# A state-space output projection by seven block products in a stage of its own, behind one chain of 32 scan chunks

## The chip, the cores and the metric

The kernel runs on one core of one Trainium2 chip. The metric is the device time of one execution in microseconds, as the median of repeated runs. All data is float32.

## The reference, cut to what matters

The program is a two-layer decoder trunk with 1,024 tokens and width 1,024. Layer 0 is attention with pooling and an FFN, layer 1 a state-space mixer (SSD) and an FFN. The change lies in the mixer of layer 1 and in what follows it:

```python
y = ssd_chunked(xs, dt, A, Bm, Cm) + xs * D[:, None]     # 8 chunks of 128 tokens, 4 groups of 8 heads
y = y.reshape(b, s, SSD_INNER) * silu(z)                  # SSD_INNER = 2048
yg = y.reshape(b, s, SSD_GROUPS, 512)
yg = yg * rsqrt(mean(yg * yg, axis=-1) + EPS)             # one root for each token and group
x = x + (yg.reshape(b, s, 2048) * norm_w) @ w_out         # the output projection, 1024 x 2048 x 1024
x = x + swiglu(rmsnorm(x, ffn_norm_w[1]), ...)            # the second FFN
```

## The kernel before, in words

**Products.** A float32 product is made of three TensorE products of float32r parts: high by high, high by low, low by high. The high part is a copy by ScalarE (`w_hi`, `y_hi`, `s_hi`, `d_hi`), the low part the difference to it, taken by GpSimd (`w_lo`, `s_lo`) or VectorE (`y_lo`, `d_lo`). The large projections (both FFNs, and the state-space input in `q_stage`) already run as seven block products in place of eight (M1 to M7: each operand is cut into 2 x 2 blocks, sums of blocks are multiplied, and each result is added to the output blocks that `ADDS_TO` names).

**Order.** Each engine has one queue of instructions, written out by hand in five blocks (SyncE, GpSimd, ScalarE, TensorE, VectorE), with semaphores between them. An instruction that waits holds all behind it on its engine.

**A group of the mixer (`ssd_group(g)`, g = 0 to 3).** `load_rows` brings back B, C (`bc_rows`) and x (`yx`) of the group, 1.5 MB in two halves of 512 tokens, from the scratch tensor `conv_rows`. The scan goes over NT = 8 chunks c. `token_major(c+1)` makes C times B (`CB`) and turns x; VectorE makes `cbm`, `btok` and `xdt` of it; GpSimd makes `xds`. TensorE then makes the states, `yoff`, and `ydiag` (L2592), for which it waits for the masked decay `mdec`. `mdec` is loaded 512 KB a chunk (`load_decay`, two buffers, behind `ydiag` of the chunk before the last), and worked on by ScalarE (`eacs`, relus, exponentials) and VectorE. VectorE adds up y (L3385, counted by `y_ready`). After each chunk TensorE makes one or two z halves (`z_half`, 12 products each, 16 a group: the gate projection of the group), ScalarE takes silu of z, VectorE multiplies it into y (`gated`).

**The projection now.** At the end of each group the gated y is squared (ScalarE), summed over four blocks (GpSimd, L1205), and over channels (`square_sums`, L2606). `split` and `lo` make `y_hi` and `y_lo`. `out_part` makes 16 output halves (8 tiles of 128 tokens, two halves of 512 columns), each of 4 blocks x 3 products (L1925 to L1927), and `add_out` (L2679) scales each by the root of its tokens and adds it to `xres`. The root is a column that fits tokens on partitions. Loads of the next group's rows and weights (`load_piece`, `w_raw`) run in this stretch. In the last group the products go in `TILE_ORDER`, and from the sixth output half on `ffn_T` puts the norm's transposes for the second FFN between them, so the tiles of x are complete one after the other.

**The down projection and the q stage**, which the new stage resembles: `down_slice` (L2298 to L2306) makes 12 products of one `s` block (`hidden`, through DRAM) and one `d` block (weights), in a ring of five buffers; its last additions (L2926) are followed by the norm (`plain`, L2691), transposes (L2003) and block sums of the q stage.

Of the kernel before, what the change touches and what calls it, by code (L numbers as in the profile page):

```python
# [33 lines left out]
P = 128  # L34
# [37 lines left out]
class Order:  # L72


    def __init__(self, names):
        self.at = {name: i + 1 for i, name in enumerate(names)}
        assert len(self.at) == len(names)
        self.total, self.seen = len(names), 0

    def count(self, layer, *name):  # L80
        return layer * self.total + self.at[name]

    def step(self, layer, *name):
        self.seen += 1
        assert self.seen == self.count(layer, *name), (self.seen, layer, name)
# [4 lines left out]
TILE_ORDER = (0, 1, 2, 4, 3, 5, 6, 7)  # L90
NEXT_PAIR = ("M2g", "M5g", "M6g", "M3g", "M7g", "M1u", "M4g", "M2u", "M5u", "M6u", "M3u", "M7u")


def trunk(nc, x, mix_norm_w, ap_w_in, ap_sinks, pool_w, pool_scale, ap_w_out, ssd_w_in, ssd_conv_w,
# [40 lines left out]
    with ExitStack() as ctx:  # L135
# [17 lines left out]
        slot5_at = [nc.sbuf_base - SPLIT_SLOTS * 4 * DM, nc.sbuf_base]  # L153
# [12 lines left out]
        scratch = small[:, 173:174]  # L166

# [22 lines left out]
        def f(ap):  # L190
# [36 lines left out]
        y_hi = at("y_hi", 0, [BG, S], F32R)  # L227

        sq = [[at(f"sq{h}{b}", b * S + BANK if h == 0 else 4 * S + b * BANK, [BANK]) for b in range(BG)]
              for h in range(2)]  # L230
        zs = [at(f"zs{b}", b % 2 * BANK, [BANK], origin=slot5_at[b // 2]) for b in range(BG)]

        yx = at("yx", 8 * S, [BG, S])
        y_lo = at("y_lo", 8 * S, [BG, S], F32R)


        def unit_at(name, unit, start, shape, dt=F32):
            return at(name, unit * DM + start, shape, dt, origin=weights_at)

# [4 lines left out]
        xs_n = [unit_at(f"xs_n{i}", 8 + i, 0, [DM]) for i in range(2)]  # L244
        bc_raw = [unit_at(f"bc_raw{i}", i, 0, [NK, P]) for i in range(2)]
# [60 lines left out]

        rows_v = at("rows_v", 0, [2 * NK, S], origin=xn_at)
        t1_val = at("t1_val", NK * S, [H2, S], origin=xn_at)
        d12 = [rows_v[:, p_, 0:BANK] for p_ in range(NP)]
        d22 = [rows_v[:, p_, BANK:] for p_ in range(NP)]  # L310
        d21 = [rows_v[:, NP + p_ % 5, p_ // 5 * BANK:(p_ // 5 + 1) * BANK] for p_ in range(NP - 1)]
# [3 lines left out]
        conv_rows = nc.dram_tensor("conv_rows", (G * NCB, P, S), F32, kind="Internal").ap()  # L315
        decay_sums = nc.dram_tensor("decay_sums", (G, NT, HG * P), F32, kind="Internal").ap()
# [15 lines left out]
        def turn_banks(layer, q):  # L332
# [310 lines left out]
        def _(sp):  # L643
# [207 lines left out]
            def ssd_group(g):  # L851
# [49 lines left out]
                if g == 0:  # L901
                    load_back(6, 7)
# [2561 lines left out]
```

## Time and profile before

| | |
|---|---|
| Median of 3 runs | 2283.26 us (2281.89 to 2283.43) |
| Profiled execution | 2282.14 us |
| Its span | 2280.4 us |
| TensorE busy | 2258.5 us, 99% |
| VectorE, ScalarE, GpSimd busy | 1320.3, 1101.5, 1320.6 us |
| Moved by DMA | 281.45 MB, mean 123 GB/s |

The span runs from the first to the last instruction that the profiler saw; the profiled execution's own time is 1.7 us longer. The ends of matmuls are modelled, so a busy TensorE need not be at its full pace. The mixer's groups lie between about 1160 and 1649 us, each 118 us apart; the second FFN follows.

### The profile page before, as it was taken

The numbers are of one execution on the slowest core, as the hardware profiler recorded it, in microseconds if no ns is written. First come the engines' busy times: TensorE is split into PE (matmuls) and PEld (weight loads), VectorE is DVE, ScalarE is ACT, GpSimd is POOL, SyncE is SP. The second block draws the span as 40 slices with busy tenths as digits, with TensorE's granted clock in tenths as the row PEclk, the third lists the DMA queues.
The fourth block names the chain that finished last, engine by engine and source line by source line (L and its number), as shares of the span: only waits on it lengthen the run. The fifth ranks groups of instructions, "written<-read, shape, count | busy, mean of one in ns | idle before, by whom it ended". The sixth has DMA issues, their size and how long they took to land.

```text
span 2280.4 us, 28960 instructions
## 1 busy us (share of the span) xinstructions
PE 2258.5 (99%) x10698; PEld 1845.5 (81%) x10698; DVE 1320.3 (58%) x1716; ACT 1101.5 (48%) x2016; POOL 1320.6 (58%) x950
## 2 busy tenths in 40 slices
PE   8999999999999999999999999999999999999998
PEld 6877888888888878888878888888888888888887
DVE  7357663333335798855568484747854343336777
ACT  4046544333333446655567474737643333334445
POOL 3224288777774664787734242334388777774654
PEclk9999999999999999999999999999999999999999
DMA  5100323323227855233263323232222323228744
GB/s 164 47 28 19 120 64 112 120 88 120 88 102 259 268 161 166 93 112 119 86 222 123 120 84 118 86 102 93 102 88 97 122 84 122 85 106 292 250 148 155
DMA packets 170807, 281.45 MB, mean 123 GB/s; under 512 B 19232, under 2 KB 104108, under 8 KB 168108
## 3 DMA queue, kind: packets, MB, share of 16 engines
q1 hardware_dynamic: 167084, 267.68, 34.9%
q10 hardware_dynamic: 3584, 11.93, 1.3%
q8 instruction: 86, 1.41, 0.3%
q14 instruction: 53, 0.43, 0.1%
HBM read 209.71 MB, written 69.86 MB: 123 GB/s over the span
## 4 chain that ended last, share of the span: by engine, by line
PE 92%; DVE 3%; POOL 2%; issue 1%; ACT 1%; DMA 1%; SPq 0%; ACTq 0%; DVEq 0%; POOLq 0%
PE ps L2212 44%; PE ps L1925 8%; PE ps L1927 8%; PE ps L1926 8%; PE ps L2302 5%; PE ps L2306 5%; PE ps L2298 5%; PE ps L2592 1%; PE ps L2582 1%; PE ps L2575 1%; PE ps L1948 1%; PE ps L2370 1%; POOL sq L1205 1%; PE ps L2135 1%; PE ps L2168 1%
## 5 line engine op out<-in xcount | busy, mean ns | idle before, releaser
L1051 POOL TENSOR_TENSOR s_lo<-s_val,s_hi 128x512 fp32r<-128x512 f32 x154 | 235.5, 1533 | 196.7 <-ACT s_hi L1575 196.0
L2862 DVE TENSOR_TENSOR xres<-ps,xres 128x512 f32<-128x512 f32 x132 | 90.5, 688 | 400.2 <-PE ps L2212 400.2
L947 POOL TENSOR_TENSOR w_lo<-w_raw,w_hi 128x1024 fp32r<-128x1024 f32 x50 | 119.3, 2387 | 270.6 <-ACT w_hi L1239 205.9
L972 POOL TENSOR_TENSOR p_lo<-p_val,p_hi 128x512 fp32r<-128x512 f32 x176 | 239.4, 1369 | 48.6 <-ACT p_hi L1380 37.5
L1380 ACT ACTIVATE p_hi<-p_val 128x512 fp32r<-128x512 f32 x176 | 111.0, 632 | 307.8 <-POOL p_val L998 307.8
L2212 PE MATMUL ps<-xn_hi,p_hi 128*128 128x512 f32 x704 | 189.0, 390 | 1.2 <-ACT xres L1483 1.2
L2212 PE MATMUL ps<-xn_lo,p_hi 128*128 128x512 f32 x704 | 188.2, 389 | 0.0
L2212 PE MATMUL ps<-xn_hi,p_lo 128*128 128x512 f32 x704 | 188.2, 389 | 0.0
L1575 ACT ACTIVATE s_hi<-s_val 128x512 fp32r<-128x512 f32 x154 | 97.0, 630 | 160.8 <-DMA d_val<-in_w_down 89.9
L1925 PE MATMUL ps<-xn_hi,w_hi 128*128 128x512 f32 x400 | 160.3, 401 | 0.0
L1926 PE MATMUL ps<-xn_lo,w_hi 128*128 128x512 f32 x400 | 156.0, 390 | 0.0
L1927 PE MATMUL ps<-xn_hi,w_lo 128*128 128x512 f32 x400 | 155.9, 390 | 0.0
L2212 PEld LDWEIGHTS ps<-xn_hi,p_hi 128*128 128x128 f32 x704 | 131.5, 188 | 28.9 <-ACT p_hi L1380 2.0
L2212 PEld LDWEIGHTS ps<-xn_lo,p_hi 128*128 128x128 f32 x704 | 132.1, 188 | 27.5
L2212 PEld LDWEIGHTS ps<-xn_hi,p_lo 128*128 128x128 f32 x704 | 132.2, 188 | 27.5
L2302 PE MATMUL ps<-d_lo,s_hi 128*128 128x512 f32 x560 | 151.3, 390 | 1.0 <-DVE d_lo L2914 0.8
L2298 PE MATMUL ps<-d_hi,s_hi 128*128 128x512 f32 x560 | 151.0, 390 | 0.0
L2306 PE MATMUL ps<-d_hi,s_lo 128*128 128x512 f32 x560 | 150.7, 389 | 0.0
L2914 DVE TENSOR_TENSOR d_lo<-rows_v,d_hi 128x512 fp32r<-128x512 f32 x108 | 126.3, 1173 | 21.7 <-ACT d_hi L1578 21.6
L1483 ACT ACTIVATE xres<-ps 128x512 f32<-128x512 f32 x132 | 77.8, 591 | 113.8 <-PE ps L2212 113.8
L1239 ACT ACTIVATE w_hi<-w_raw 128x1024 fp32r<-128x1024 f32 x48 | 50.0, 1051 | 159.9 <-PE ps L1927 154.4
L2302 PEld LDWEIGHTS ps<-d_lo,s_hi 128*128 128x128 f32 x560 | 104.7, 188 | 24.6 <-DVE d_lo L2914 3.1
(361 smaller groups left out, 5570.3 us busy)
## 6 DMA issues: line engine op xcount, KB each, us to landing
s_val<-hidden SPq DMA_DIRECT2D x154, 256.0 KB, 2.9
hidden<-xres SPq DMA_DIRECT2D x20, 1792.0 KB, 6.5
wv_g<-in_w_gate SPq DMA_DIRECT2D x22, 1024.0 KB, 5.2
wv_u<-in_w_up SPq DMA_DIRECT2D x20, 1024.0 KB, 5.1
d_val<-in_w_down SPq DMA_DIRECT2D x70, 256.0 KB, 4.1
rows_v<-in_w_down SPq DMA_DIRECT2D x64, 256.0 KB, 3.8
mdec<-decay_sums SPq DMA_DIRECT2D x32, 512.0 KB, 4.2
xres<-parked_x SPq DMA_DIRECT2D x24, 512.0 KB, 6.0
```

The costliest lines, as they stand in the source:

```text
L947: pool.tensor_tensor(w_lo[piece.slot][:, :], raw[piece.raw][:, :], f(w_hi[piece.slot][:, :]), ALU.subtract).then_inc(lo_done, 1)
L972: pool.tensor_tensor(p_lo[n][:, :, :], src, f(p_hi[n][:, :, :]), ALU.subtract).then_inc(p_lo_done, 1)
L1051: pool.tensor_tensor(s_lo[i][:, :], s_val[i][:, :], f(s_hi[i][:, :]), ALU.subtract)\
L1380: act.activation(p_hi[n][:, :, :], src, ACT.Copy).then_inc(p_hi_done, 1)
L1925: pe.matmul(dst, l_hi, r_hi, start=first, stop=False, skip_group_check=reopened)
L1926: pe.matmul(dst, l_hi, r_lo, start=False, stop=False, skip_group_check=reopened)
L1927: return pe.matmul(dst, l_lo, r_hi, start=False, stop=last, skip_group_check=reopened)
L2212: ins = pe.matmul(bank, l_[:, k, :], r_[:, k, :], start=first and k == 0, stop=last and k == H2 - 1, skip_group_check=reopened)
L2298: pe.matmul(banks[t_], s_hi[i][:, t_ * P:(t_ + 1) * P], d_hi[i][:, :], start=p == 0, stop=False)
L2302: pe.matmul(banks[t_], s_hi[i][:, t_ * P:(t_ + 1) * P], d_lo[i][:, :], start=False, stop=False)
L2306: pe.matmul(banks[t_], s_lo[i][:, t_ * P:(t_ + 1) * P], d_hi[i][:, :], start=False, stop=False)\
L2914: dve.tensor_tensor(d_lo[i][:, :], down_operand(DOWN[j], p, i), f(d_hi[i][:, :]), ALU.subtract).then_inc(d_lo_done, 1)
```

## The change

- **Products.** The projection moves behind all four groups. It is made of seven block products of eight pairs of blocks (`OUT_SEQ`, 56 slices of 12 products, `out_slice`). The token blocks are two halves of 512 tokens, the channel blocks pairs of 128, the columns two halves of 512.
- **y through DRAM.** The root is now applied before the projection: `square_sums` makes it as four rows of 128 tokens, `root_row` stores the 2 KB row and loads it back as 128 x 512 (`rr`), `row_normed` multiplies, `mix` makes the four sums of blocks on VectorE (S1 to S4), and `store_blocks` writes the seven kinds of y block to `gated_y` (14 stores of 256 KB a group). `load_out` loads each slice's y block and weight block (one to three loads of 256 KB) into a ring.
- **One chain of 32 chunks.** `token_major(k+1)` of the next group stands in the last chunk of the group before. Gates, norms, sums and stores of a group lie in the next group's chunks; those of the last group lie behind chunk 31, while slices 0 to 8 (M1 and M2 of other groups' blocks) are at TensorE. z goes in other orders, two to three halves after each chunk, and none after the last.
- **x.** It stays parked in DRAM through the mixer and comes back in eight loads of 512 KB (`load_x_back`) during the first slices.
- **Entry into the second FFN.** `second_entry` and `second_T` put the norm's first four transposes between slices of M3, and the other four between products of the FFN. Tiles 4 to 7 are complete after the last slice.
- The q stage's semaphores are merged with the FFN's (`q_full` into `product_full`, and so on), with the same waits.

```diff
-        ssd_slots = [[0, 3, 1, 2, 4, 0, 3, 1], [2, 0, 1, 3, 4, 2, 0, 1], [3, 0, 1, 2, 4, 3, 0, 1], [2, 1, 3, 0, 4, 2, 1, 3]]
+        ssd_slots = [[0, 3, 1, 2]] * G
+        OUT_SEQ = ([(0, p) for p in range(6)] + [(1, p) for p in range(3)] + [(0, p) for p in (6, 7)]
+                   + [(1, p) for p in range(3, NO)] + [(j, p) for j in range(2, 7) for p in range(NO)])
+        Z_AFTER_CHUNK = [[(5,), (6, 7), (8,), (9,), (10, 11), (12, 13), (14,), (15,)],
+                         [(0, 1), (2, 3), (4, 5), (6, 7), (8, 9), (10, 11), (12, 13), (14, 15)],
+                         [(0, 1), (2, 3), (4, 5), (6, 7), (8, 9), (10, 11), (12, 13), (14, 15)],
+                         [(0, 1, 2), (3, 4), (5, 6), (7, 8), (9, 10), (11, 12, 13), (14, 15), ()]]
@@ SyncE @@
+            def load_decay(k):
+                g, c = k // NT, k % NT
+                if k >= 2:
+                    sp.wait_ge(ydiag_full, k - 1)
+                sp.dma_start(mdec[c % 2]..., decay_sums...).then_inc(decay_loaded[c % 2], 16)
+            def root_row(n):
+                sp.wait_ge(rms_ready, n + 1)
+                sp.dma_start(rr_rows[n], rinv[0:4, :]).then_inc(rr_stored, 16)
+                sp.wait_ge(rr_stored, 16 * (n + 1))
...
+                sp.dma_start(rr[n % 2][:, :], rr_rows[n:n + 1]...to_broadcast([P, BANK])).then_inc(rr_loaded, 16)
+                load_piece(g, 3)
+                for c in range(NT):
+                    if NT * g + c + 2 < NT * G:
+                        load_decay(NT * g + c + 2)
+                    if c == 0 and g:
+                        root_row(2 * g - 2)
...
+                    if c == 2 and g:
+                        first_stores(g - 1)
...
+                    if c == 4 and g:
+                        sp.wait_ge(y_stored, 16 * (14 * (g - 1) + 4))
+                        root_row(2 * g - 1)
...
+                    if c == 6:
+                        if g:
+                            sp.wait_ge(y_normed, BG * 2 * g)
+                            store_blocks(g - 1, "M1", "M2")
+                            sp.wait_ge(mix_ready, 8 * (g - 1) + 4)
+                            store_blocks(g - 1, "M7")
+                        else:
+                            sp.wait_ge(gc_ready, 1)
+                        if not last:
+                            load_xrows(g + 1, 0)
+                            load_bc(g + 1, 0)
+                            load_piece(g + 1, 2)
+                    if c == 7:
+                        if g:
+                            sp.wait_ge(mix_ready, 8 * g)
+                            store_blocks(g - 1, "M6", "M3")
+                            sp.wait_ge(y_stored, 16 * 14 * g)
+                        if not last:
+                            load_xrows(g + 1, 1)
+                            sp.wait_ge(ydiag_full, NT * (g + 1))
+                            load_bc(g + 1, 1)
+            def out_loads(load_gate):
+                for s_ in range(2, 6):
+                    load_out(s_)
+                load_x_back(4)
+                load_out(6)
+                load_out(7)
+                load_x_back(0)
+                root_row(2 * G - 2)
+                load_x_back(5)
+                first_stores(G - 1)
+                sp.wait_ge(y_stored, 16 * (14 * (G - 1) + 4))
+                root_row(2 * G - 1)
+                load_out(8)
+                load_x_back(1)
+                sp.wait_ge(y_normed, BG * (2 * G - 1) + 2)
+                store_blocks(G - 1, "M1")
+                sp.wait_ge(y_stored, 16 * (14 * (G - 1) + 6))
+                load_out(9)
...
@@ TensorE @@
+            def token_major(k):
+                g, c = k // NT, k % NT
+                if c % 4 == 0:
+                    pe.wait_ge(rows_loaded[c // 4], 32 * (g + 1))
...
+                for c in range(NT):
+                    k, tok = NT * g + c, slice(c * P, (c + 1) * P)
+                    if k + 1 < NT * G:
+                        token_major(k + 1)
...
+            for s_ in range(OUTS):
+                out_slice(s_)
+                if s_ == 3:
+                    square_sums(2 * G - 1)
+                if o_at(6, 2) <= s_ <= o_at(6, 5):
+                    second_T(s_ - o_at(6, 2))
@@ the second FFN, TensorE @@
                 product(0, "M1g")
+                    second_T(4)
                 product(0, "M2g")
+                    second_T(5)
+                    second_T(6)
                 product(0, "M1u")
+                    second_T(7)
                 product(0, "M2u")
                 product(0, "M5g")
@@ VectorE @@
+                for c in range(NT):
+                    masked_decay(c)
+                    if k + 1 < NT * G:
+                        token_major(k + 1)
+                    if c == 0 and g:
+                        gated(g - 1, 1)
+                        reciprocal_rms(2 * g - 2)
+                    if c == 2 and g:
+                        for b in range(BG):
+                            row_normed(g - 1, b, 0)
+                        for i in range(2):
+                            mix(g - 1, "S1", i)
+                    if c == 4:
+                        gated(g, 0)
+                        if g:
+                            reciprocal_rms(2 * g - 1)
+                    if c == 6 and g:
+                        for b in H1_ORDER:
+                            row_normed(g - 1, b, 1)
+                        for i in range(2):
+                            mix(g - 1, "S3", i)
+                    if c == 7 and g:
+                        for name in ("S2", "S4"):
+                            for i in range(2):
+                                mix(g - 1, name, i)
+                    if c >= 6 and last:
+                        out_low(c - 6)
...
+            gated(G - 1, 1)
+            reciprocal_rms(2 * G - 2)
+            out_low(2)
+            out_low(3)
+            for b in range(BG):
+                row_normed(G - 1, b, 0)
+            for i in range(2):
+                mix(G - 1, "S1", i)
+            out_low(4)
+            reciprocal_rms(2 * G - 1)
+            out_low(5)
+            for b in H1_ORDER:
+                row_normed(G - 1, b, 1)
+            for name in ("S3", "S2", "S4"):
+                for i in range(2):
+                    mix(G - 1, name, i)
+            ffn(1)
@@ VectorE, end of second_entry @@
+                    for t_ in range(4):
+                        add_result("M3", t_, 4, 1)
+                    for q in range(4, NT):
+                        make(q)
+                    for i in range(4):
+                        tail_t1(i)
+                        tail_t2(i)
+                        tail_t3(i)
+                        tail_b22(i)
+                    for i in range(4):
+                        tail_lo1(i)
+                    for i in range(4):
+                        tail_t4(i)
+                        tail_lo2(i)
```

## Rows read from the trace of the kernel before

**Rows 1.** The page's head and busy times of the engines.

```profile
span 2280.4 us, 28960 instructions
...
PE 2258.5 (99%) x10698; PEld 1845.5 (81%) x10698; DVE 1320.3 (58%) x1716; ACT 1101.5 (48%) x2016; POOL 1320.6 (58%) x950
```

**Rows 2.** Windows: us, busy us (x instructions) of PE, PEld, DVE, ACT, POOL, PEclk, DMA share, GB/s.

```profile
1252.00:1370.00 118.00, 117.47 (x654) 95.86 (x653) 72.74 (x128) 68.60 (x136) 42.36 (x27) 1.00 0.30 99
...
1291.00:1349.00 58.00, 58.00 (x382) 46.65 (x381) 42.84 (x86) 44.18 (x91) 24.49 (x17) 1.00 0.37 122
...
1606.00:1713.00 107.00, 106.31 (x504) 87.95 (x503) 72.57 (x87) 59.23 (x109) 66.44 (x47) 1.00 0.26 91
```

**Rows 3.** Groups of instructions, TensorE, 1252.2 to 1370.3: busy us, mean ns, idle before.

```profile
L1925 PE MATMUL ps<-w_hi,y_hi 128*128 128x512 f32 x65 | 25.6, 394 | 0.0
...
L2606 PE MATMUL ps<-small,sq 128*128 128x1 f32 x16 | 2.0, 246 | 0.5 <-POOL sq L1205 0.5
```

**Rows 4.** The chain of work, 350 to 700: start, us, what.

```profile
350.21 348.42 PE ps L2212 x1536
```

**Rows 5.** The chain of work, 1290 to 1350: ydiag of chunks 1 and 2.

```profile
1302.05 1.02 PE ps L2592 x16
...
1311.26 1.02 PE ps L2592 x16
```

**Rows 6.** Timeline, VectorE, 1347 to 1356: start, us, operation.

```profile
1351.04 3.97 DVE L3396 SCALAR_TENSOR_TENSOR y_lo<-yx,gconst,y_hi 128x512 fp32r<-128x512 f32 x3
1354.93 0.68 DVE L3334 TENSOR_TENSOR yx<-ps,yx 128x512 f32<-128x512 f32 x1
1355.53 0.68 DVE L3334 TENSOR_TENSOR yx<-zs,yx 128x512 f32<-128x512 f32 x1
```

**Rows 7.** Timeline, ScalarE, 1315 to 1323.

```profile
1316.82 1.28 ACT L1837 ACT_TABLE_LOAD   x1
...
1318.11 1.27 ACT L1837 ACTIVATE eacs<-mdec 64x512 f32<-64x512 f32 x2
...
1321.90 1.16 ACT L1849 ACTIVATE mdec<-mdec 128x512 f32<-128x512 f32 x2
```

**Rows 8.** Timeline, GpSimd, 1345 to 1358.

```profile
1350.80 2.99 POOL L1205 TENSOR_TENSOR sq<-sq,sq 128x512 f32<-128x512 f32 x2 [7.77 <-ACT sq L1871]
```

**Rows 9.** DMA issues by line: KB each, median us to landing.

```profile
s_val<-hidden SPq DMA_DIRECT2D x154, 256.0 KB, 2.9
...
xres<-parked_x SPq DMA_DIRECT2D x24, 512.0 KB, 6.0
...
yx<-conv_rows SPq DMA_DIRECT2D x8, 1024.0 KB, 6.8
...
parked_x<-xres ACTq DMA_DIRECT2D x16, 512.0 KB, 2.6
...
decay_sums<-sumT ACTq DMA_DIRECT2D x1, 128.0 KB, 2.4
```

**Rows 10.** Timeline, SyncE's queue, 799 to 800.

```profile
799.68 0.43 SPq L739 DMA_DIRECT2D rows_v<-in_w_down  x1
```

**Rows 11.** Windows, as in rows 2, of 3 us each.

```profile
745.00:748.00 3.00, 3.00 (x15) 2.49 (x14) 3.00 (x3) 1.47 (x4) 2.54 (x2) 1.00 0.91 341
...
907.00:910.00 3.00, 3.00 (x19) 2.61 (x18) 1.13 (x1) 2.04 (x4) 0.00 (x0) 1.00 0.99 302
```

**Rows 12.** Timelines, VectorE, 914 to 925 and 944 to 957.

```profile
915.01 2.73 DVE L2926 TENSOR_TENSOR xres<-ps,xres 128x512 f32<-128x512 f32 x4
...
917.85 1.28 DVE L2691 SCALAR_TENSOR_TENSOR xs_n<-xres,small,norm_wp 128x1024 f32<-128x1024 f32 x1
...
919.24 1.28 DVE L2691 SCALAR_TENSOR_TENSOR xs_n<-xres,small,norm_wp 128x1024 f32<-128x1024 f32 x1
...
948.25 6.83 DVE L3070 TENSOR_TENSOR comb_lo<-comb_val,comb_hi 128x512 fp32r<-128x512 f32 x4
```

**Rows 13.** Timeline, ScalarE, 914 to 918.

```profile
916.55 0.29 ACT L1256 ACTIVATE small<-small 128x1 f32<-128x1 f32 x1
```

More of the change, by code:

```diff
@@ L837, in load_piece @@
             def load_piece(g, k):
[L838 to L842 removed]
+                load(Piece(SSD0 + g * GP + k), blocks[:, :, g * BG + zc + k, :])
             ffn(0)
             q_stage()
[L847 to L849 removed]
@@ L901, in ssd_group @@
-                if g == 0:
-                    load_back(6, 7)
-                t.add("chunk", NT)
-                t.add("out", 2 * NT)
-            t = Tally(chunk=0, out=2 * NT)
+                    if c == 5 and last:
+                        load_out(1)
+                    if c == 6:
[4 more added lines that the diff above has]
+                            store_blocks(g - 1, "M7")
+                        else:
+                            sp.wait_ge(gc_ready, 1)
[3 more added lines that the diff above has]
+                            load_piece(g + 1, 2)
@@ L1468, in ffn, with first_entry @@
-                tail_hi1(2)
-                tail_first(3)
-                tail_hi1(3)
-                tail_hi2(2)
+                def first_entry():
+                    for q in range(6):
+                        if q >= 3:
+                            xhi(TILE_ORDER[q - 3])
+                        park_and_square(q)
+                        if q == 2:
+                            p_hi_of(0, "M1g")
+                        if q == 3:
+                            p_hi_of(0, "M2g")
+                        if q == 4:
+                            p_hi_of(0, "M5g")
+                    tail_first(0)
+                    tail_hi1(0)
+                    xhi(3)
+                    park_and_square(6)
+                    tail_hi2(0)
+                    tail_hi3(0)
+                    tail_first(1)
+                    park_and_square(7)
+                    tail_hi1(1)
+                    tail_first(2)
+                    p_hi_of(0, "M1u")
+                    tail_hi2(1)
+                    p_hi_of(0, "M2u")
+                    p_hi_of(0, "M6g")
+                    p_hi_of(0, "M3g")
+                    tail_hi1(2)
+                    tail_first(3)
+                    tail_hi1(3)
+                    tail_hi2(2)
@@ L2222, in product @@
                         if mn == "M1g":
-                            turn_free(layer, 4)
+                            turn_free(layer, 3 if layer else 4)
+                        elif mn == "M1u" and layer:
+                            pe.wait_ge(out_added, o_add_order.count(0, "M3", 3, 4, 1))
                         elif mn == "M1u":
@@ new lines, in z_half @@
+            def z_half(g, i):
+                n = i // 2
+                u, (b, half) = ZU * g + n, Z_ORDER[g][n]
+                piece = in_group(g)(b)
+                if i % 2 == 0:
+                    if b not in [b_ for b_, _ in Z_ORDER[g][:n]]:
+                        pe.wait_ge(lo_done, piece.count(1))
+                    if u >= 3:
+                        pe.wait_ge(z_done, u - 2)
+                ins = columns(z_bank(u), piece, half, range(i % 2 * NK // 2, (i % 2 + 1) * NK // 2))
+                if i % 2:
+                    ins.then_inc(z_full, 1)
```

1267 lines of the change are left out of this document (771 added, 496 removed), and 2 rows, old and new, of the table comb_hi_order.

## The prediction

> **What bounds the kernel now.** I read the page's head first: TensorE is busy 99% of the span, every other engine under 60% [rows 1]. Then the stages in windows: one state-space group takes 118 us and TensorE works all but 0.5 us of it, at full clock; the 107 us with the last projection and the entry into the second FFN lack 0.7 us [rows 2]. A busy TensorE need not be at its pace, so I took the pace from the chain of work: 1,536 products in 348.42 us are 0.2268 us each [rows 4]. In the group's own window 192 z products and 192 output products are 87.1 us; the scan's small matmuls are most of the rest. The one true wait is 0.5 us before the square sums [rows 3]. So the order of the queues hides the gates, norms, splits and loads wholly. VectorE at 73 and ScalarE at 69 of 118 us have room. The reader is to see that work removed from TensorE is worth its full time, and that a new wait costs its full time too.
>
> **What the change takes away.** Now the projection is 768 products: 64 of each of three kinds a group ([rows 3] show one kind, with one more at the window's edge), four groups. Seven block products over eight pairs of blocks are 56 slices x 12 = 672. 96 fewer x 0.2268 = 21.8 us. The z products, the scan's matmuls, the 64 transposes for the second FFN and the eight square-sum matmuls stay in number. The 0.5 us wait at the end of three groups goes too, 1.6 us. Together -23.4 us.
>
> **Scan chain, per chunk.** A chunk with two z halves lasts 9.2 us [rows 5], 5.4 of it z, 3.7 the chunk. ScalarE spends 4.9 us on a chunk's exponentials and relus (1318.1 to 1323.1) and the group adds some 26 us (silus, squares, splits, ten table loads of 1.28) [rows 7]: 65 of 74 us. VectorE is busy 42.8 us in the 58 of eight chunks [rows 2]; gates, row norms and block sums add 24 operations a group, 0.6 us apart from start to start where GpSimd is idle (two gates) and 1.3 where it runs beside them (three y_lo) [rows 6, 8]: 57 to 74 of 74 us. These mostly fit, with the six operations of chunk 2 or 6 the densest: 3.7 to 7.8 us stand ahead of that chunk's state, where about 4 us are free. Together with the turn from M1 to M5, where three loads a slice come, I take 1 us, between 0 and 5.
>
> **Group turn-over.** This is what I think decides. token_major of the next group's chunk 0 now stands in chunk 7's turn, and waits for both rows_loaded transfers. SyncE issues them in its turn 6, behind load_decay, which waits until ydiag of chunk 6 is full. From that moment TensorE has only the z halves of chunk 6 before it reaches the wait: one half (2.7 us) in group 0, two (5.4) in groups 1 and 2. The rows need longer. bc_rows and yx, 1.5 MB, now land 6.8 us after the second issue [rows 9], about 7.2 after the first.
> Group 0: the decay load (0.5 MB) goes first. At the 300 GB/s that the fullest stretches show [rows 11], 2.1 MB are 7.0 us, 0.9 for what one load has beyond its bytes (512 KB land in 2.6 us, 1.7 of it bytes) [rows 9], 0.4 for the issue: 8.3, less 2.7 = 5.6 us of stall; 4.9 if the decay load costs nothing.
> Groups 1 and 2: SyncE also waits there for four row norms and two S3 sums on VectorE (0.3 and 1.5 us after ydiag at 0.6 each) and issues six stores of 256 KB, 0.4 each [rows 10], ahead of the rows. 3.7 MB are 12.2 us, +1.3 as in group 0 = 13.5, less 5.4 = 8.1 us. If the rows are not held up by the stores' bytes: 3.0 + 7.2 - 5.4 = 4.8. If VectorE runs at 1.3, the rows are issued 2.5 us later: 10.6.
> Sum 5.6 + 8.1 + 8.1 = 21.8 us, between 14 and 27. Before, the projection's 43.5 us of products lay over these loads. The z halves, stage sums and everything else on TensorE queue behind the waiting instruction.
> The Trainium skill (DMA: Bandwidth & Descriptors, Anatomy of one DMA) gives a transfer 2.0 us plus its bytes at 436 GB/s; by it the wait in groups 1 and 2 would be about 5.4 us each, and the sum 5 us lower. The fullest windows here show 302 to 341 GB/s, so I stay with them.
>
> **The tail of the last group.** Nothing lies behind chunk 31 but slices. Slices 0 to 5 (16.3 us), the square sums and the first four products of slice 6 end 18.1 us after the last ydiag. Slice 6 then wants d_lo, and out_low(6) stands on VectorE behind all norms and sums of the last group. Its chain, from the last ydiag (0):
> VectorE still has four sums (group 2's S2 and S4) and out_low(1) ahead of y: y at +4.6, four gates to +7.1. SyncE stores those sums, waits until they have landed (+5.1 to 5.7), and only then issues load_out(2): slice 2 gets its splits at +10, so 5 us are lost there already. Fourteen issues of 0.4 [rows 10] end at +11. Then root_row(6): store 2.4 (as decay_sums), load 2.9 (as s_val) [rows 9] and issues, +17. Four norms, two sums: +21. SyncE stores M4 and M5, waits: +25. root_row(7): +31. Four norms, six sums, out_low(6): +37.7. Slice 6 ends at +39.5 where without waits it ends at +19.9: 19.6 us. That is with an idle queue. But 4.2 MB were issued ahead of root_row(6), and [rows 9] show 6.0 us for 512 KB behind two others against 2.6 alone: if the small store waits for its place, its row comes 7 to 8 us later, 28 us in all. I take the middle, 24.
> By the Trainium skill (DMA: Bandwidth & Descriptors, Queues, rings and completion order) each DMA engine takes a ring's descriptors in their order; by that this term is 28 and the sum 4 us more. No row here shows a small transfer behind a backlog.
>
> **Entry into the second FFN.** Before, the norm and transposes lay among output products, with 0.7 us lost [rows 2]. Now tiles 4 to 7 get their last addition after the last slice. Rows of the entry into the q stage give the steps: four additions 2.7, the first tile's square and root done 1.8 after they begin, norms 1.4 apart [rows 12, 13]; sums take 0.6 as the gates do [rows 6]. There 96 products hid them; here it is M1g, M2g, M1u, M2u, 48. From the last slice (0): transpose 5 ends at 7.4, norm 7 waits for it and ends at 8.8, tile 4's four operations end at 11.3, and transpose 6 waits for them: 3.9 us. M5g waits 0.9 for tile 7 and 0.7 to 3.3 for its low parts, M6g 2.3 to 7.3 for T2's: the eight operations before it take 0.6 each alone, 1.7 beside GpSimd [rows 12], which splits weights there. 8 to 15 us; I take 11, since GpSimd is busy part of it.
>
> **Sum.** 2282.1 (the profiled execution, 1.7 beyond its span; the three runs' median is 2283.3) - 23.4 + 21.8 + 24 + 11 + 1 = 2316.5 us.
>
> **Rivals.**
> Main, 0.45: as summed, 2316.
> Short transfers, 0.24: every term but the scan's at its low end, 14.5 + 20 + 8: 2301. For it: rows of loads that met an idle queue. Against: the fullest stretches already carry 256 KB slices only.
> Queues and the shared pace of VectorE and GpSimd, 0.15: 27 + 28 + 15 + 5 = 75: 2334.
> The tail hides itself (the slices before M1 of the last blocks do cover it), 0.06: 2293.
> The other side, transfers, 0.10: if rows and small hops are there when wanted, the turn-over costs nothing and the tail is only VectorE's operations after root(7), which end at +20, just in time: -23.4 + 11 + 1, 2271. It decides once turn-over and tail together are under 11.4 us, against 46 in my sum. Against it: the row loads took 6.8 us where little else was on the queue [rows 9].
> That the products do not fall by 96 I exclude: the loops fix the count.
>
> **Range and chances.** The middle three cases span 2301 to 2334; I reach down to 2292 for the tail's case and up to 2337, which leaves the faster case and about 1 in 10 more outside. A difference under 0.2% (4.6 us) is no difference that this kernel's runs can tell. Faster by more 0.10, within 0.04, slower 0.86.
>
> **What would show it.** Right: TensorE idle for 5 us or more at CB of chunks 8, 16 and 24, ended by a load of yx or bc_rows; in slice 6, ended by VectorE's d_lo; at slice 2, by the load; at the second FFN's transpose 6 and M6g; 96 products fewer, still 0.2268 apart. Wrong if the gap between chunk 7's z and chunk 8 is under 2 us, or if slice 6 follows slice 5 without a gap. What would spoil the number most: row loads that are quicker than the stores ahead of them, or a scan in which VectorE falls behind chunk by chunk.

## The result and the profile after

The changed kernel takes 2367.2 us (median of 4 runs, 2364.6 to 2368.9), the kernel before 2282.9: ratio 1.037, interval 1.035 to 1.039. I had predicted 2316 with a range to 2337. The sign is right and the size is not: +84 us where my sum had +34.

First the page of the changed kernel, the rows that answer to [rows 1], and its row of granted clock in 40 slices:

```profile
span 2366.9 us, 29286 instructions
...
PE 2267.5 (96%) x10602; PEld 1841.8 (78%) x10602; DVE 1425.3 (60%) x1828; ACT 1146.5 (48%) x2101; POOL 1373.0 (58%) x992
...
PEclk9999999999999999999999989889999999999999
```

The 96 products are gone (10698 to 10602), yet TensorE is busy 9 us longer. Fewer products take longer, and the clock row says why: parts 24, 26 and 27 of its 40 are not at full clock, while all of the kernel before's were. The same in windows over the stages (columns as in [rows 2]: length, busy time of PE, PEld, DVE, ACT, POOL, granted clock, DMA share, GB/s), for groups 1 and 3, the tail of the last group, the turn from M1 to M5, and the entry into the second FFN:

```profile
1238.00:1323.00 85.00, 73.90 (x449) 58.83 (x449) 68.29 (x115) 65.57 (x128) 33.34 (x23) 0.96 0.44 147
...
1413.00:1503.00 90.00, 87.26 (x511) 69.60 (x513) 71.94 (x122) 63.12 (x122) 31.05 (x23) 0.94 0.38 129
1503.00:1563.00 60.00, 37.61 (x137) 28.94 (x134) 31.22 (x42) 14.67 (x26) 22.95 (x13) 0.74 0.63 221
1563.00:1591.00 28.00, 19.67 (x78) 14.23 (x77) 17.80 (x26) 8.81 (x15) 10.75 (x8) 0.93 0.80 287
...
1708.00:1748.00 40.00, 26.66 (x115) 21.16 (x115) 35.50 (x46) 24.59 (x51) 16.11 (x11) 0.87 0.34 129
```

TensorE lacks 11 of 85 us in group 1 and 22 of 60 in the tail, and the clock is below 1.00 wherever it lacks much (and in group 3, which begins behind a long wait). VectorE is now busy 80% of group 1 (62% in [rows 2]) and 89% of the entry. What TensorE waits for, by its weight loads (PEld: us in total, times, longest):

```profile
PEld ps L2864 <- DMA bc_rows<-conv_rows: 21.5, 3, 7.8
PEld ps L2909 <- DVE od_lo L3747: 19.8, 4, 10.0
...
PEld ps L2974 <- DVE mdec L3835: 9.9, 6, 2.3
```

Now one of these waits closely: the turn from group 0 to 1, in windows. TensorE goes idle at 1232.8, work resumes at 1238.4:

```profile
1235.00:1238.00 3.00, 0.00 (x0) 0.00 (x0) 0.00 (x0) 2.95 (x10) 0.62 (x1) 0.58 1.06 392
1238.00:1239.00 1.00, 0.62 (x3) 0.62 (x4) 0.00 (x0) 1.00 (x1) 0.00 (x0) 0.50 0.94 285
1239.00:1242.00 3.00, 3.00 (x16) 2.78 (x16) 1.19 (x4) 0.27 (x1) 0.95 (x1) 0.50 0.06 16
1242.00:1243.00 1.00, 1.00 (x16) 0.93 (x16) 0.68 (x1) 0.00 (x0) 0.10 (x1) 0.83 0.00 0
```

The clock falls to 0.50, the 1.2 GHz level, while the engine is idle, and stays there for some 4 us after the data have come. What that costs I count as (1 - clock) times busy time: 2.0 us here. Done in this way for every microsecond from 1150 to 1830, beside the gaps over 0.4 us of the timeline, the ledger of the changed kernel is:

| Place | gaps | low clock | my sum had |
|---|---|---|---|
| Turn-over of groups, 3 | 20.2 (5.6, 7.4, 7.2) | 7.0 | 21.8 |
| Tail: slices 2, 4, 6 | 22.4 (4.3, 9.5, 8.5) | 8.6 | 24 |
| Chunks, 7 waits | 10.5 | 3.4 | } 1 |
| Turn from M1 to M5 | 8.1 | 2.0 | } |
| Entry into the FFN | 16.4 | 3.8 | 11 |
| Later | 0.6 | | |
| Sum | 78.2 | 24.8 | 57.8 |

103.0, less 2.2 of such gaps before and 21.8 of products, is 79.0 us; the first ydiag starts 1.8 us later than before; the spans differ by 86.5. Of the 5.7 us left about 4 are the gaps' own measure: a product's modelled end lies 0.16 us behind the start of the next one (0.39 against 0.2268), and there are 24 gaps. The last 2 us I can't place. The ledger is an account: it says how long TensorE was idle or slow, not what each item would give back if it went, for low clock ahead of a wait whose end hangs on another engine only shortens that wait.

### The profile page after: what moved, and what is told of

Read it like the earlier page. It is cut to its first block, busy times and chain, and to the rows that moved or that the text cites. A ratio compares the mean times of both kernels' runs of the same rounds, so it can differ in the third digit from the quotient of the medians.

```text
span 2366.9 us, 29286 instructions
## 1 busy us (share of the span) xinstructions
PE 2267.5 (96%) x10602; PEld 1841.8 (78%) x10602; DVE 1425.3 (60%) x1828; ACT 1146.5 (48%) x2101; POOL 1373.0 (58%) x992
## 4 chain that ended last, share of the span: by engine, by line
PE 84%; DVE 7%; DMA 3%; issue 2%; POOL 2%; SPq 1%; ACT 1%; DVEq 0%; ACTq 0%; POOLq 0%
PE ps L2525 42%; PE ps L2228 5%; PE ps L2230 5%; PE ps L2229 5%; PE ps L2617 5%; PE ps L2621 5%; PE ps L2613 5%; PE ps L2909 1%; PE ps L2913 1%; PE ps L2905 1%; PE ps L2251 1%; PE ps L2974 1%; PE ps L2694 1%; DMA bc_rows<-conv_rows 1%; PE ps L2957 1%
## 5 line engine op out<-in xcount | busy, mean ns | idle before, releaser
L1143 POOL TENSOR_TENSOR w_lo<-w_raw,w_hi 128x1024 fp32r<-128x1024 f32 x34 | 81.5, 2401 | 195.4 <-ACT w_hi L1471 108.7
L1397 POOL TENSOR_TENSOR os_lo<-os_val,os_hi 128x512 fp32r<-128x512 f32 x56 | 89.7, 1608 | 106.9 <-ACT os_hi L2135 106.7
```

## The experiments

All times are medians of four runs. "Ledger" is the sum of gaps and low clock as above.

**What an idle costs beyond its length.** Theory A: the clock falls in an idle stretch, and the work behind it pays. This is measured where nothing else can be late, in the FFNs of the kernel before.

```diff
+ if (layer, p + 1) in GAPS:                       # SyncE, 8 places
+     sp.wait_ge(product_full, product_order.count(layer, p + 1, "M2g"))
+     sp.dma_start(gap_dst, ssd_w_in[0][0:P, 0:2 * DM]).then_inc(gap_done, 16)
+ pe.wait_ge(gap_done, 16 * (...))                 # TensorE, ahead of M5g
```

> The kernel before, with eight waits put into the two FFNs where TensorE otherwise never waits (before M5g of pairs 2, 4, 6 and 8): each waits for a 1 MB copy from DRAM to DRAM that SyncE issues when product M2g is done. The output is untouched. Nothing else can be late there, so whatever the kernel gains in time beyond the eight gaps is the price of having been idle. The gaps should be 5 to 8 us each, 40 to 64 us. Theory A (the granted clock falls in an idle stretch and comes back only some us after work resumes): the time exceeds 2283 plus the gaps by 2 to 3 us for each, 16 to 24 us in all. Theory B (an idle costs its own length): 2283 plus the gaps, within 4 us.

Measured: 2350.0 us, ratio 1.030 (1.028 to 1.031), 67.1 more than before. The waits, and windows around one of them, then the work behind it:

```profile
PE ps L2218 <- DMA gap_dst<-in_ssd_w_in: 46.6, 8, 6.1
```

```profile
1764.00:1765.00 1.00, 0.00 (x0) 0.00 (x0) 1.00 (x2) 0.00 (x0) 1.00 (x2) 0.91 1.04 434
1765.00:1766.00 1.00, 0.00 (x0) 0.00 (x0) 0.51 (x1) 0.00 (x0) 1.00 (x1) 0.50 0.72 225
1766.00:1771.00 5.00, 4.72 (x11) 3.79 (x12) 0.00 (x0) 0.00 (x0) 0.03 (x1) 0.50 0.90 279
1771.00:1772.00 1.00, 1.00 (x4) 0.76 (x4) 0.00 (x0) 0.23 (x1) 0.12 (x1) 0.68 1.07 459
```

```profile
1766.28 2.04 PE L2218 MATMUL ps<-xn_hi,p_hi 128*128 128x512 f32 x4 [5.21 <-DMA gap_dst<-in_ssd_w_in]
```

Four products take 2.04 us where they take 1.07. 46.6 us of gaps leave 20.5, 2.6 for each idle of 5 to 6 us; the low clock by windows adds up to 21.0. Theory A. The rival within it, that the copies' traffic is the cause, falls with the same waits filled:

```diff
+ for _ in range(20):    # ahead of the same wait; M5g overwrites the result
+     pe.matmul(bank, xn_hi[:, 0, 0:P], xn_hi[:, 0, 0:BANK], start=True, stop=True)
```

> The kernel before with the same eight waits for a 1 MB copy, but TensorE fills the first 4.5 us of each with 20 products whose result is overwritten by the product behind. The length of each wait is the same, only TensorE is busy in most of it. In the run without the filling the eight waits had 46.6 us of idle time and the kernel took 67.1 us more than before. Theory A (being idle costs a low clock afterwards): the granted clock stays at 1.00 and the time comes down to 2283 + 47, about 2330. Theory B (the 20 us beyond the gaps come from somewhere else, such as the copies' traffic or late weights): it stays near 2350.

Measured: 2330.2 us, ratio 1.021 (1.019 to 1.023). The filling takes 4.70 us of one wait and 0.71 is left, and the mean clock of the whole run is 0.999:

```profile
1749.25 4.70 PE L2270 MATMUL ps<-xn_hi 128*128 128x512 f32 x20
...
1754.65 1.20 PE L2218 MATMUL ps<-xn_hi,p_hi 128*128 128x512 f32 x4 [0.71 <-DMA gap_dst<-in_ssd_w_in]
```

The waits are as long as before and 20 us are back. That is the low clock's price, shown.

**The same filling in the changed kernel.**

```diff
+ warm((20, 28, 28)[g], z_bank(u), xn_hi[:, 0, 0:P], xn_hi[:, 0, 0:BANK])   # ahead of token_major(8 (g + 1))
+ if s_ in (2, 4, 6):                                                      # ahead of out_slice(s_)
+     warm({2: 16, 4: 36, 6: 32}[s_], ps[:, 0, :], os_hi[0][:, 0:P], od_hi[0][:, :])
```

> The changed kernel with 160 products added whose results are overwritten: 20, 28 and 28 just ahead of the waits at the three group turn-overs, 16, 36 and 32 ahead of output slices 2, 4 and 6. They fit into the six longest waits (5.6, 7.4, 7.2, 4.3, 9.5, 8.5 us). Theory A (each long wait costs its gap and then some 5 to 6 us of products at the 1.2 GHz level): the rows at a granted clock of 0.50 behind these six waits add up to 15.6 us, so the kernel comes down by 12 to 16 us, to about 2353, with the clock at 1.00 there and the data no earlier than before. Theory B (the low clock behind a wait costs nothing, since the next data would be late anyway): no change, 2367, within 2 us, or slower.

(In group 0 the filling also overwrites the first half of the last z product, so that block is not the reference's.) Measured: 2364.5 us, 2.7 faster, outside both theories' bounds and nearest to theory B. The four times of this kernel (2362.6 to 2366.9) overlap those of the changed one (2364.6 to 2368.9), so even the 2.7 is hardly clear of noise. The clock did stay at 1.00 in the first five places. But gaps fell by only 29.7 us for 36.3 us of filling, and the low clock from 24.8 to 15.4, not by 15.6: it fell instead at a 2.1 us wait in chunk 5 of group 1 where it had not, and behind slice 6. And the waits of the tail do not end when TensorE is ready, so being earlier only made the next one longer: slice 6 waited 3.8 us behind 7.3 of filling, 11.1 in all, where it had waited 8.5. So low clock is paid in full only where the end of the next wait hangs on TensorE. Ledger 2.8 less, measured 2.7.

**Turn-over.** What SyncE does in the changed kernel at the turn from group 1 to 2, chunk 6's ydiag ending at 1310.7, and VectorE ahead of it:

```profile
1310.78 0.32 SPq L933 DMA_DIRECT2D mdec<-decay_sums  x1
1313.48 1.79 SPq L954 DMA_DIRECT2D gated_y<-yx  x4
1315.32 0.96 SPq L954 DMA_DIRECT2D gated_y<-mix_S  x2
1316.32 0.56 SPq L890 DMA_DIRECT2D yx<-conv_rows  x1
```

```profile
1308.60 4.85 DVE L3802 SCALAR_TENSOR_TENSOR yx<-yx,gconst,rr 128x512 f32<-128x512 f32 x4
1313.38 1.28 DVE L3821 TENSOR_TENSOR mix_S<-yx 128x512 f32<-128x512 f32 x2
```

The rows are issued 5.6 us after that ydiag and TensorE goes on at 1323.9.

```diff
  for c in range(NT):
+     if c == 6 and not last:
+         sp.wait_ge(mix_ready, 8 * (g - 1) + 4)      # group 0: gc_ready
+         load_xrows(g + 1, 0)
+         load_bc(g + 1, 0)
      load_decay(...)
```

> The changed kernel, but SyncE issues the next group's first rows in turn 6 ahead of the load of the decay sums and ahead of the six stores. Theory A (the order of the issues and the bytes ahead set the turn-over): the wait of group 0 to 1 (5.6 us and 2.0 us of low clock) goes, those of groups 1 and 2 (7.4 and 7.2 us, 5 us of low clock together) fall to about 3 us each, in all 16 to 20 us faster, about 2349. Theory B (the transfer's own time from VectorE's last sum on sets it): only 0.4 us for each issue and group 0's decay load, 3 us faster, 2364.

Measured: 2357.5 us, 9.7 faster, between the two theories. Group 0's wait went with its low clock. Those of groups 1 and 2 fell to 5.0 and 5.1, not 3, with 3.0 us of low clock behind each: the norms, 1.2 us each with GpSimd's split of a weight beside half of them, held the rows back until 4 us after ydiag. Then the same with B's and C's rows a turn earlier and one z half ahead of the waiting transposes:

```diff
+     if c == 5 and g and not last:
+         load_bc(g + 1, 0)
+ if c == NT - 1 and 0 < g < G - 1:                   # TensorE
+     z_half(g, Z_AFTER_CHUNK[g][c][0])
  token_major(k + 1)
```

> The changed kernel with the rows issued first, as in the run of that name, and besides B's and C's rows a turn earlier and, in groups 1 and 2, one of the last two z halves (2.7 us) ahead of the waiting transposes instead of behind ydiag of chunk 7. Theory A (what stands ahead of the rows and how much work lies over them sets the wait): after the run with the rows first, whose waits were 5.0 us each, they fall to 1 to 2 us with little low clock behind, 8 to 12 us faster than that run, about 2347. Theory B (the z half is only moved from one wait to another: chunk 0's mask then comes late instead): 2355 to 2358.

Measured: 2345.5 us, ratio 1.027 (1.026 to 1.029), 21.7 faster than the changed kernel. The waits there are 0.6 and 0.7 us, no low clock behind them, and 0.6 to 0.8 at the next chunk; in group 2 the wait at chunk 2 grew from 0.9 to 2.1 us, with 1.7 of low clock. Theory A: 21.7 of the turn-over's 27.2 us were a matter of what stands ahead of a transfer and over it.

**Tail.** The rows behind the last chunk in the changed kernel, TensorE first:

```profile
1513.57 2.04 PE L2905 MATMUL ps<-od_hi,os_hi 128*128 128x512 f32 x4 [4.34 <-ACT od_hi L2138]
...
1533.33 2.08 PE L2909 MATMUL ps<-od_lo,os_hi 128*128 128x512 f32 x4 [9.53 <-DVE od_lo L3747]
...
1550.37 2.08 PE L2909 MATMUL ps<-od_lo,os_hi 128*128 128x512 f32 x4 [8.52 <-DVE od_lo L3747]
```

VectorE, between two waits for the row of roots:

```profile
1526.97 4.38 DVE L3802 SCALAR_TENSOR_TENSOR yx<-yx,gconst,rr 128x512 f32<-128x512 f32 x4 [9.05 <-DMA rr<-rr_rows]
1531.38 1.29 DVE L3821 TENSOR_TENSOR mix_S<-yx 128x512 f32<-128x512 f32 x2
1532.60 0.68 DVE L3747 TENSOR_TENSOR od_lo<-od_val,od_hi 128x512 fp32r<-128x512 f32 x1
```

SyncE: store of the roots, and load of the row once the store has landed, twice.

```profile
1516.18 0.50 SPq L939 DMA_DIRECT2D rr_rows<-rinv  x1
1523.02 0.33 SPq L945 DMA_DIRECT2D rr<-rr_rows  x1
1538.54 0.26 SPq L939 DMA_DIRECT2D rr_rows<-rinv  x1
1539.71 0.33 SPq L945 DMA_DIRECT2D rr<-rr_rows  x1
```

A store of 2 KB takes 6.8 us behind fourteen loads and 1.2 with the queue empty.

```diff
- for s_ in range(2, 6): load_out(s_) ... load_out(6), load_out(7) ... root_row(2 * G - 2)
+ load_out(2), load_out(3)                 # in chunk 31's turn, ahead of the last stores of group 2
+ load_out(4), load_out(5), root_row(2 * G - 2), load_out(6), load_out(7)
- norms and S1; out_low(4)                 # VectorE
+ out_low(4); norms and S1; ... out_low(6), (7), (8) ahead of the second norms
```

> The changed kernel, but behind the last chunk the small store of the roots is issued ahead of the backlog of loads, the loads of slices 2 and 3 ahead of the last stores of group 2, and VectorE makes the low parts of slices 4 and 6 to 8 ahead of the norms that wait for the row of roots. Theory A (these slices wait in a queue for nothing that they need): the gaps of slices 2, 4 and 6 (22.4 us and 8.6 us of low clock) go, and one wait of 5 to 10 us comes back at the slice of the last group's first block (slice 9), whose chain through the two rows of roots is real: 20 to 26 us faster, about 2344. Theory B (the chain through DRAM sets the stage's length whatever stands ahead): the stall moves to slice 9 whole, 3 us faster, 2364.

Measured: 2362.7 us, 4.5 faster, ledger 7.7. Near theory B. The waits of slices 2 to 6 fell to 6.7 us, but slice 9, the last group's first block, waited 6.6 and slice 13 another 3.0; in all 16.3 us. From the last ydiag (1503.3) to the row of that block in SBUF (1544.7) are 41 us, of which nine slices cover 24.5. That leaves 16.5, and the waits up to that block are 13.4, with 1.7 of low clock between them. So the tail is about as long as its chain. The next run shortens the chain and lays more over it.

```diff
- OUT_SEQ = (0, 0..5), (1, 0..2), (0, 6), (0, 7), (1, 3..7), ...
+ OUT_SEQ = (0, 0..5), (1, 0..5), (0, 6), (0, 7), (1, 6), (1, 7), ...
- first_stores(G - 1); wait for them; root_row(2 * G - 1)
+ root_row(2 * G - 1); first_stores(G - 1)
```

> The changed kernel with its tail put in another order: besides the edits of the run with the tail's order, the second row of roots is made and loaded before the first stores of the last group instead of behind them, slices (1, 3) to (1, 5) stand ahead of the last group's first blocks, and M1's additions stand six and six behind (1, 6) and (1, 7). Theory A (the tail is as long as the chain from the last ydiag over gate, square sum, root, row through DRAM, norm, store and load, 41 us in the earlier run of which nine slices cover 24.5; shorten it and lay twelve slices over it): chain 33 to 35 us against 32.7 of slices, so of the tail's 31 us of waits and low clock about 6 stay, 20 to 28 us faster than the changed kernel, about 2343. Theory B (the queue's traffic sets it, 31 transfers of 256 to 512 KB in this stretch): not under 2355.

Measured: 2354.9 us, 12.3 faster, half of what theory A gave and at theory B's bound (not under 2355), so the time does not part the two. Up to slice 14 it went nearly as A said: 7.8 us of waits and 3.0 of low clock (A: about 6 of both), where the run before had 16.3 and 6.2. Then slice (1, 7) waited for its low part. I took the additions of M1's result for the cause, here and for the last run; but VectorE is done with the six ahead at 1558.8. It then idles for the weights of the next slice, whose sum it takes first, and that load stood behind six loads of the residual:

```profile
1567.30 0.77 PE L2233 MATMUL ps<-od_hi,os_hi 128*128 128x512 f32 x1 [12.19 <-DVE od_lo L3753]
```

```profile
1565.86 0.69 DVE L3739 TENSOR_TENSOR rows_v<-rows_v,od_val 128x512 f32<-128x512 f32 x1 [7.02 <-DMA od_val<-in_ssd_w_out]
```

**Chunks.** In chunk 4 four gates and a reciprocal stand ahead of the state; chunk 5's mask is then late, and TensorE waits 2.1 us for it:

```profile
1289.13 3.33 DVE L3791 TENSOR_TENSOR yx<-zs,yx 128x512 f32<-128x512 f32 x4
1292.38 0.93 DVE L3796 RECIPROCAL rinv<-rinv 4x128 f32<-4x128 f32 x1
...
1295.22 2.95 DVE L3894 SCALAR_TENSOR_TENSOR yx<-yx,gconst,eacs 128x128 f32<-128x128 f32 x4
1298.10 2.35 DVE L3835 TENSOR_TENSOR mdec<-mdec,cbm 128x512 f32<-128x512 f32 x2
```

```diff
- c == 4: gated(g, 0);          c == 0 and g: gated(g - 1, 1)
+ c == 4: gated(g, 0, (0, 1));  c == 0 and g: gated(g - 1, 1, (0, 1))
+ c == 5: gated(g, 0, (2, 3));  c == 1 and g: gated(g - 1, 1, (2, 3))
```

> The changed kernel, but the four gates of each half stand in two chunks (two and two) on VectorE instead of in one. Theory A (four more operations between two masks make that chunk's masked decay late): the waits of about 2.1 us in chunk 5 (and 1.7 us of low clock behind two of them) and of 1.2 us in chunk 2 shrink, 5 to 9 us faster, about 2360. Theory B (VectorE has no room in these groups): the wait goes to the next chunk, within 2 us of 2367.

Measured: 2375.7 us, 8.5 slower: a miss for both. The waits of chunks 1 and 5 are gone (chunk 1's is the one of 1.2 us that the text above puts in chunk 2). But in each of groups 1 to 3 GpSimd's product `xds` for chunk 2's state is late by 4.3 to 5.1 us. VectorE's `xdt` for it has been there since 1257.9. What GpSimd still has to do first is a split of a weight and the sums of squares, and both come later because ScalarE's squares, which stand ahead of that weight on ScalarE, wait 3.5 us for the moved gates:

```profile
1269.54 2.04 PE L2957 MATMUL ps<-xds,btok 128*128 128x512 f32 x2 [5.01 <-POOL xds L1426]
```

```profile
1263.21 4.74 POOL L1405 TENSOR_TENSOR sq<-sq,sq 128x512 f32<-128x512 f32 x3
1267.91 1.49 POOL L1426 TENSOR_TENSOR xds<-xdt,gconst 128x512 f32<-128x512 f32 x1
```

So only the half in chunks 4 and 5 may be split; that half goes into the last runs.

**Turn from M1 to M5, and entry.** The two longest of three waits for M1's additions (the third is 1.5 us), and the entry's two longest:

```profile
1587.01 0.76 PE L2905 MATMUL ps<-od_hi,os_hi 128*128 128x512 f32 x1 [3.09 <-DVE xres L3761]
1590.61 0.80 PE L2905 MATMUL ps<-od_hi,os_hi 128*128 128x512 f32 x1 [2.83 <-DVE xres L3761]
...
1720.01 1.78 PE L2251 MATMUL ps<-ident,xs_f 128*128 128x128 f32 x8 [4.14 <-DVE xn_lo L3135]
...
1743.41 2.08 PE L2525 MATMUL ps<-comb_lo,p_hi 128*128 128x512 f32 x4 [7.20 <-DVE comb_lo L3151]
```

```diff
- if (j, p) == (1, 7): quota = 8
+ if j == 1 and p >= 4: quota = 4
```

> The changed kernel, but the 16 additions of product M1's result stand four at a time behind slices (1, 4) to (2, 1) on VectorE instead of eight, four and four from (1, 7) on. Theory A (M5's banks wait only for additions that stand too late in the order): the waits of 1.5, 3.1 and 2.8 us at the turn from M2 to M5 go, with 2.0 us of low clock, 7 to 9 us faster, about 2359. Theory B (the additions cannot begin before the last blocks are stored, which is shortly before): 0 to 3 us faster.

Measured: 2358.2 us, 9.0 faster. The three waits are gone; theory A. At slice (1, 7) the wait is now 2.6 us instead of 0.7, with 1.7 of low clock.

```diff
- make(4..7); tails 0..3; low parts; T4 sums
+ make(4..6); tail 0; make(7); tails 1, 2; T4 sums 0, 1; tail 3; low parts; ...
```

> The changed kernel, but in the entry into the second FFN VectorE does tile 4's four operations before the norm of tile 7 (which waits for a transpose) and two of the T4 sums in an idle moment before tile 7's operations. Theory A (the order on VectorE sets the wait before transpose 6): that wait (4.1 us, with 1.7 us of low clock behind it) nearly goes and the 7.2 us wait in M6g loses 2 to 3 us, together 6 to 9 us faster, about 2359. Theory B (VectorE's total work sets when M6g can go on): transpose 6 comes earlier and M6g waits as much longer; 2 to 3 us faster, 2364.

Measured: 2363.2 us, 4.0 faster, between the two. Transpose 6 waits 0.5 us instead of 4.1, but M5g then waits 2.4 instead of 0.6 before its first pass, and M6g 5.7 instead of 7.2: VectorE has nothing to spare there.

**All together.**

> The changed kernel with all reorderings together: the tail's chain, the rows issued early and covered, the entry's order, and of the gates only those of the first half split over chunks 4 and 5. No work is added or taken away. Theory A (the places are independent, each wait with its low clock): 2367 less about 24, 22, 4 and 8, some 2309. Theory B (they share VectorE and the queue, and a wait that is taken away comes back at the next place): not under 2325. Neither theory lets it fall under the kernel before (2283), since the entry's waits and the chunks' stay.

Measured: 2322.2 us, ratio 1.017 (1.015 to 1.019), 45.0 faster than the changed kernel; gaps 46.2, low clock 9.8 us. Short of A's 58 by 13, the wait of 12.5 at slice (1, 7) again. The last run aims at that one, as a matter of M1's additions:

```diff
- OUT_SEQ = ..., (1, 0..5), (0, 6), (0, 7), (1, 6), (1, 7)
+ OUT_SEQ = ..., (1, 0..4), (0, 6), (0, 7), (1, 5), (1, 6), (1, 7)
- the rows of the residual behind load_out(15)
+ two of them behind load_out(14)
```

> The run with all reorderings, but for its one long wait, the 12.5 us at slice (1, 7), which stood there because its low part was queued on VectorE behind additions of M1's result that waited for the last stores and for the rows of the residual. Now (0, 6) and (0, 7) stand ahead of (1, 5) to (1, 7), so that three slices (8.2 us) lie over those additions, and the residual's rows are loaded two pairs earlier. Theory A (that wait was a place in a queue): 12.5 us and 1.5 to 2.5 us of low clock become 2 to 5 us of waits, 8 to 11 us faster, 2311 to 2314, the best version of the change. Theory B (the blocks of the last group are stored that late whatever the order, and the result's additions with them): within 3 us of 2322.

Measured: 2321.5 us, the same: theory B by the number. The wait at slice (1, 7) fell from 12.5 to 7.4 us, but waits of 0.8 and 2.4 stand at the two slices ahead of it now, and the low clock of the run is 14.8 us. Windows over the tail (1524 to 1544), then VectorE's wait:

```profile
1524.00:1529.00 5.00, 3.99 (x17) 2.74 (x16) 1.19 (x2) 1.15 (x2) 1.11 (x2) 1.00 1.05 404
1529.00:1534.00 5.00, 2.79 (x11) 1.61 (x10) 0.75 (x1) 0.95 (x2) 0.45 (x2) 1.00 1.03 369
1534.00:1539.00 5.00, 4.57 (x12) 3.27 (x12) 4.77 (x7) 1.35 (x3) 2.32 (x2) 0.66 1.05 407
1539.00:1544.00 5.00, 0.00 (x0) 0.00 (x0) 0.16 (x1) 0.00 (x0) 0.00 (x0) 0.74 1.05 404
```

```profile
1544.83 0.69 DVE L3759 TENSOR_TENSOR rows_v<-rows_v,od_val 128x512 f32<-128x512 f32 x1 [5.67 <-DMA od_val<-in_ssd_w_out]
```

The DMA engines are full for 20 us. Stores, slices' loads and 3 MB of the residual share them, and the load for which VectorE waits, issued about 1535, lands 9.9 us later. That bytes are the bound here is argued from this and not shown, because in all three runs with this tail an order was left as it was: VectorE sums the next slice's weights first and takes the low part of (1, 7) behind that. ScalarE had its high part 7 us earlier:

```profile
1537.45 0.61 ACT L2152 ACTIVATE od_hi<-rows_v 128x512 fp32r<-128x512 f32 x1
```

```profile
1545.44 0.68 DVE L3773 TENSOR_TENSOR od_lo<-rows_v,od_hi 128x512 fp32r<-128x512 f32 x1
```

With the low part ahead of the sum, slice (1, 7) could run inside the wait: 12 products, 2.7 us and the low clock on them, as an estimate. No run tests it, nor a load of the next slice's weights ahead of the residual.

The ledger holds over all of these runs. Against the changed kernel it gives -2.8 (filled), -11.0 (rows first), -7.7 (tail's order), +7.0 (gates), -5.0 (entry), -6.6 (additions), -22.4 (rows covered), -14.5 (tail's chain), -47.0 and -45.6 (all); the spans give -1.7, -10.9, -8.2, +5.7, -5.6, -8.0, -22.0, -17.0, -47.2 and -42.9. No reordering reached the kernel before: the best is 37.7 us above it, ratio 1.016 (1.014 to 1.018).

## Why the prediction was right in sign and wrong in size

**What the change takes away: right.** 96 products fewer, at full clock still 0.2268 us apart.

**Group turn-over: place and releaser right, the size in groups 1 and 2 by luck.** 20.2 us of gaps for 21.8. In those two groups two errors met: the rows were issued 5.6 us after ydiag where I had 3.0, for the norms took 1.2 us each, which I had kept as the bound; and they landed 7.5 us later where I had 10.5. The second comes from the rate. The 302 to 341 GB/s of [rows 11] are not the fullest windows of the kernel before, as the prediction has it; over 20 us this one moves 386:

```profile
720.00:740.00 20.00, 20.00 (x90) 16.56 (x89) 11.03 (x12) 8.08 (x14) 8.24 (x7) 1.00 1.02 386
```

At that rate 3.7 MB take 9.5 us and not 12.2 (an estimate from this row). The Trainium skill's figure that the prediction set beside its own (DMA: Bandwidth & Descriptors, Anatomy of one DMA) is a fit to transfers that GpSimd issues; these are SyncE's.

**Tail: 4 us too small, one place missed.** The gaps are 22.4 us for 24, but TensorE ran slow between them and so used up part of the delay. By the time slice 6 had its low part, 22.4 us of gaps and 5.6 of low clock had gone by: 28.0, which is the upper side of my fork and not its middle. I had slice 6 alone behind the norms; slice 4 stands behind them too and took half of it. The fork about the small store is settled by 6.8 us behind the backlog against 1.2. By the Trainium skill (DMA: Bandwidth & Descriptors, Queues, rings and completion order) descriptors of a ring are taken in order; these two rows agree.

**Entry: too small.** 16.4 us of gaps, against 11 with 8 to 15 as its bounds. VectorE was busy 89% of these 40 us; M6g's 7.2 is the upper end that I gave it, and 3.0 us of waits for transposes and norms before it had no term.

**The step that failed first: "a new wait costs its full time too".** A wait that the engine spends idle costs its time and the low clock behind it: 24.8 us in the ledger of the changed kernel, and my sum has no term for it. Without the 5.6 us that are part of the tail's 28 it is 19.2, still the largest part of the miss. The runs with idles put into the kernel before measured it alone: 2.6 us for an idle of 5 to 6, given back whole when the same waits are filled. In the changed kernel itself the price is read from the ledger only: the run that filled its six longest waits gave back 2.7 us. In the kernel before the clock falls only behind the last product, where there is no work to slow, so the price could not be read there. The Trainium skill (TensorE: Matmul & The Clock Gate, HAM oscillation) says that a wait for data that is long enough puts TensorE back to half the clock, so that the work behind it starts slow; the windows agree (0.50 behind each long gap). It was a rule that spoke against this change, and I did not weigh it.

**The second: "these mostly fit ... I take 1 us, between 0 and 5"** for the scan and the turn from M1 to M5. They took 18.6 us of gaps and 5.4 of low clock. I had compared sums, 57 to 74 us of VectorE in 74. But a chunk's mask is due every 9 to 10 us, and five operations ahead of it (four gates and a reciprocal) delay it however idle the engine is later: 2.1 us at chunk 5 three times, 1.2 at chunk 1 twice. The six operations of chunks 2 and 6, which I had called the densest, made no mask late. The other two waits, 0.9 us at chunk 2 twice, are GpSimd's `xds`, for which I had no term. The sixteen additions, which I did not count at all, take 9.8 us, and little more than one slice stands over them. Moving only these additions brought 9.0 us back.

In sum: low clock 19.2, scan and M1 to M5 17.6, entry 5.4, tail 4.0, less 1.6 where the turn-over was too high, and 7.5 of small or unplaced terms (the 1.8 us before the first ydiag and the 5.7 beyond the ledger among them): 52.1. That is the miss in the profiled executions, +86.5 us against +34.4. The rivals failed with the main case, since all of them priced a wait at its length.

## What to carry to other kernels

Price a new wait of several microseconds on a full TensorE as its length plus the low clock behind it (2.6 us here for 5 to 6 of idle), unless work can be laid over most of it, or the end of the next wait hangs on another engine anyway. Where the work of an engine is moved between deadlines, compare it with each deadline, not with the engine's total. And before reordering a queue ask whether its chain or its bytes set the end: order gave 22 us at the turn-over, where 1.5 MB were wanted; the one other order tried in the last run's tail, where the DMA engines were full, gave nothing.

## What the runs showed of the hardware

- Two waits of the same length need not cost the same: of the 2.1 us waits at chunk 5 in the changed kernel, the first has 1.00 behind it and the two others 1.7 us of low clock each. In the run with the filling the first one had it too (1.6 us).
- The DMA engines moved 369 to 407 GB/s over 20 us (the last run's tail), and 386 over 20 us in the kernel before (720 to 740), which is more than the 302 to 341 of [rows 11].
- The same DMA of 2 KB lands after 1.2 us or 6.8, by what was issued ahead of it.
